# The light expert's folds one chunk later, and the job table made between the first gathers' rounds

## The reference, cut to what matters

```python
logits = (xt @ w_router).astype(jnp.float32)
top_v, top_i = lax.top_k(logits, TOP_K)            # 2 of 8
gates = jax.nn.softmax(top_v, axis=-1)
gate = jnp.sum(jax.nn.one_hot(top_i, N_EXPERTS) * gates[..., None], axis=1)
y = jnp.zeros_like(xt)
for e in range(N_EXPERTS):
    y = y + gate[:, e:e + 1] * ((jax.nn.silu(xt @ wg[e]) * (xt @ wu[e])) @ wd[e])
```

## Time and profile before

| | |
|---|---|
| median of 3 runs | 1616.9 us (1615.19 to 1618.0) |
| the profiled execution's own time | 1615.04 us |
| its span in the trace | 1613.2 us |
| PE busy | 1531.5 us, 95% |
| DVE busy | 1300.9 us, 81% |
| ACT busy | 1088.7 us, 67% |
| moved by DMA | 462.70 MB |
| expert pairs | from about 657 us to the end of the span |

### The profile page before, as it was taken

The page is one execution under the profiler, slowest core; times in us unless marked ns, Lnnn a source line. Parts: engine busy times, 40 slices in busy tenths (PEclk is TensorE's granted clock), DMA queues, the critical chain, the costliest instruction groups (busy, mean ns, idle before and its releaser), DMA issues.

```text
span 1613.2 us, 20830 instructions
## 1 busy us (share of the span) xinstructions
PE 1531.5 (95%) x7379; PEld 1257.6 (78%) x7379; DVE 1300.9 (81%) x1600; ACT 1088.7 (67%) x1423; POOL 119.8 (7%) x242
## 2 busy tenths in 40 slices
PE   6999999999999997799999899999999999999995
PEld 5888888888888886687777677787777787777884
DVE  5786676475554657689999999999999999999998
ACT  4664564645443463378888788878788877788884
POOL 3433332001000101000000000000000000000000
PEclk9999999999999999799999999999999999999998
DMA  9537444436465644399999999999999999999994
GB/s 344 201 131 218 147 139 150 170 98 216 144 200 179 212 134 145 99 319 383 383 388 398 362 380 386 387 364 401 381 385 386 393 362 397 366 386 387 397 377 182
DMA packets 203076, 462.70 MB, mean 287 GB/s; under 512 B 7902, under 2 KB 12396, under 8 KB 202844
## 3 DMA queue, kind: packets, MB, share of 16 engines
q1 hardware_dynamic: 200304, 454.32, 78.0%
q0 software_dynamic: 1904, 5.38, 1.3%
q10 hardware_dynamic: 764, 1.66, 0.3%
HBM read 460.29 MB, written 1.05 MB: 286 GB/s over the span
## 4 chain that ended last, share of the span: by engine, by line
PE 78%; ACT 8%; DVE 6%; issue 3%; DVEq 2%; DMA 2%; SPq 0%; ACTq 0%
PE ps L2027 8%; PE ps L2028 8%; PE ps L2029 8%; PE ps L2483 7%; PE ps L2485 7%; PE ps L2484 7%; PE ps L2498 7%; PE ps L2499 7%; ACT whi_sb L919 5%; PE ps L2536 4%; DVE wlo_sb L1268 2%; DMA raw_sb<-w_in 2%; PE ps L2445 1%; ACT gate_l_sb L1208 1%; PE ps L2073 1%
## 5 line engine op out<-in xcount | busy, mean ns | idle before, releaser
L1268 DVE TENSOR_TENSOR wlo_sb<-raw_sb,whi_sb 128x1024 fp32r<-128x1024 f32 x672 | 785.8, 1220 | 56.4 <-ACT whi_sb L919 52.4
L919 ACT ACTIVATE whi_sb<-raw_sb 128x1024 fp32r<-128x1024 f32 x672 | 668.0, 1051 | 178.6 <-PE ps L2499 88.3
L1260 DVE TENSOR_TENSOR wlo_sb<-raw_sb,whi_sb 128x1024 fp32r<-128x1024 f32 (+2 forms) x198 | 230.2, 1203 | 138.4 <-ACT whi_sb L911 137.3
L911 ACT ACTIVATE whi_sb<-raw_sb 128x1024 fp32r<-128x1024 f32 (+2 forms) x198 | 192.2, 1022 | 158.8 <-PE ps L2029 129.5
L2027 PE MATMUL ps<-whi_sb,xlo_sb 128*128 128x512 f32 (+2 forms) x544 | 212.4, 390 | 3.8 <-DVE xlo_sb L1307 3.4
L2029 PE MATMUL ps<-whi_sb,xhi_sb 128*128 128x512 f32 (+2 forms) x544 | 208.3, 383 | 0.0
L2028 PE MATMUL ps<-wlo_sb,xhi_sb 128*128 128x512 f32 (+2 forms) x544 | 208.2, 383 | 0.0
L2498 PE MATMUL ps<-whi_sb,xhi_sb 128*128 128x512 f32 x448 | 180.9, 404 | 0.0
L2483 PE MATMUL ps<-whi_sb,xlo_sb 128*128 128x512 f32 x448 | 177.4, 396 | 0.9 <-DVE xlo_sb L1818 0.7
L2499 PE MATMUL ps<-wlo_sb,xhi_sb 128*128 128x512 f32 x448 | 175.7, 392 | 0.0
L2485 PE MATMUL ps<-whi_sb,xhi_sb 128*128 128x512 f32 x448 | 175.3, 391 | 0.0
(11 more groups left out here) (378 smaller groups left out, 2109.6 us busy)
## 6 DMA issues: line engine op xcount, KB each, us to landing
raw_sb<-moe_wg SPq DMA_DIRECT2D x115, 1024.0 KB, 7.6
raw_sb<-moe_wu SPq DMA_DIRECT2D x112, 1024.0 KB, 7.6
raw_sb<-moe_wd SPq DMA_DIRECT2D x112, 1024.0 KB, 7.7
raw_sb<-w_in SPq DMA_DIRECT2D x40, 1024.0 KB, 5.1
raw_sb<-w_out SPq DMA_DIRECT2D x16, 1024.0 KB, 5.1
raw_sb<-ffn_wg SPq DMA_DIRECT2D x10, 1024.0 KB, 5.1
raw_sb<-ffn_wu SPq DMA_DIRECT2D x10, 1024.0 KB, 5.2
raw_sb<-ffn_wd SPq DMA_DIRECT2D x10, 1024.0 KB, 5.1
```

The lines of the kernel that those rows point to most:

```text
L911: nc.scalar.activation(whi[i % SPLIT][:, c:c + k // 2, 0:n], raw[i % RAW][:, c:c + k // 2, 0:n], ACT.Copy).then_inc(hi_ready, 1)
L919: nc.scalar.activation(whi[i % SPLIT][:, c:c + KC // 2, :], raw[i % RAW][:, c:c + KC // 2, :], ACT.Copy).then_inc(hi_ready, 1)
L1260: op = V.tensor_tensor(wlo[i % SPLIT][:, c:c + k // 2, 0:n], raw[i % RAW][:, c:c + k // 2, 0:n], whi[i % SPLIT][:, c:c + k // 2, 0:n], ALU ...
L1268: op = V.tensor_tensor(wlo[i % SPLIT][:, c:c + KC // 2, :], raw[i % RAW][:, c:c + KC // 2, :], whi[i % SPLIT][:, c:c + KC // 2, :], ALU.su ...
```

## The change

The folds of the light job move one step later, and with them what follows: the gate's fold from one to two steps after its last chunk, its silu from two to three, the value's fold from one to two, the product from two to three and the split from three to four. The heavy job's turn stays at one step, under the name `turn_h`. The gathers for the next pair start at step `up_end` + 5 instead of + 4; in the first pair this takes the heavy output's scatter, which comes at the earliest two steps after the last gather, from step 76 to 77. In ACT's code the silu stands ahead of the value's copy. `kinds`, `extras` and `table` leave the iterations of the first pair and go between the copies of the first gathers' rounds.

```diff
-Plan = namedtuple("Plan", "steps gate value fold_g silu_l after_value product_l split_l y_out pick gather back scat_l scat_h")
+Plan = namedtuple("Plan", "steps gate value turn_h fold_g silu_l fold_u product_l split_l y_out pick gather back scat_l scat_h")
...
-    gather = {up_end + 4 + r: r for r in range(ROUNDS)}
+    gather = {up_end + 5 + r: r for r in range(ROUNDS)}
     scat_h = max(min(y_out) + 2, max(gather) + 2)
-    return Plan(steps, both("g"), both("u"), ends(LIGHT_JOB, "g", 1), ends(LIGHT_JOB, "g", 2), both("u", 1),
-                ends(LIGHT_JOB, "u", 2), ends(LIGHT_JOB, "u", 3), y_out, up_end + 1, gather, LEAD if first else 6,
+    return Plan(steps, both("g"), both("u"), ends(HEAVY_JOB, "u", 1), ends(LIGHT_JOB, "g", 2), ends(LIGHT_JOB, "g", 3),
+                ends(LIGHT_JOB, "u", 2), ends(LIGHT_JOB, "u", 3), ends(LIGHT_JOB, "u", 4), y_out, up_end + 1, gather, LEAD if first else 6,
                 None if first else 1, scat_h)
...
-            for r in range(ROUNDS):
-                gathered(0, r)
-
...
+
+            kinds()
+            gathered(0, 0)
+            extras()
+            for r in range(1, ROUNDS):
+                gathered(0, r)
+            table()
...
                     if first(j):
-                        if i == 0:
-                            kinds()
-                        if i == 1:
-                            extras()
-                        if i == 2:
-                            table()
```

More of the change, by code:

```diff
@@ L231, in ends, with both @@
                 if s.b == b and s.chunk.which == which and s.chunk.last}
-    def both(which, later=0):
-        return tuple(ends(b, which, later) for b in (HEAVY_JOB, LIGHT_JOB))
+    def both(which):
+        return tuple(ends(b, which) for b in (HEAVY_JOB, LIGHT_JOB))
     up_end = max(max(ends(b, "u")) for b in (HEAVY_JOB, LIGHT_JOB))
     y_out = {i: b for b in (HEAVY_JOB, LIGHT_JOB) for i in ends(b, "d")}
-    gather = {up_end + 4 + r: r for r in range(ROUNDS)}
+    gather = {up_end + 5 + r: r for r in range(ROUNDS)}
     scat_h = max(min(y_out) + 2, max(gather) + 2)
-    return Plan(steps, both("g"), both("u"), ends(LIGHT_JOB, "g", 1), ends(LIGHT_JOB, "g", 2), both("u", 1),
-                ends(LIGHT_JOB, "u", 2), ends(LIGHT_JOB, "u", 3), y_out, up_end + 1, gather, LEAD if first else 6,
+    return Plan(steps, both("g"), both("u"), ends(HEAVY_JOB, "u", 1), ends(LIGHT_JOB, "g", 2), ends(LIGHT_JOB, "g", 3),
+                ends(LIGHT_JOB, "u", 2), ends(LIGHT_JOB, "u", 3), ends(LIGHT_JOB, "u", 4), y_out, up_end + 1, gather, LEAD if first else 6,
                 None if first else 1, scat_h)
@@ L1197, in pair @@
                         nc.scalar.activation(act_h[:, :], acc[:, HEAVY_JOB, 0, :], ACT.Silu).then_inc(hg_silu, 1)
-                    if i in plan.after_value[HEAVY_JOB]:
-                        p = plan.after_value[HEAVY_JOB][i]
+                    if i in plan.turn_h:
+                        p = plan.turn_h[i]
                         act.wait_ge(hT_ps, done + p + 1)
@@ L1208, in pair @@
                         nc.scalar.activation(gate_l[:, :], acc[:, LIGHT_JOB, 0, :], ACT.Copy).then_inc(lg_copied, 1)
+                    if i in plan.silu_l:
+                        p = plan.silu_l[i]
+                        act.wait_ge(lgT_ps, done + p + 1)
+                        if not first(j) or p:
+                            act.wait_ge(l_lo, done + p)
+                        nc.scalar.activation(actT_l[:, :], l_tp(p)[0], ACT.Silu).then_inc(l_silu, 1)
                     if i in plan.value[LIGHT_JOB]:
@@ L1214, in pair @@
                         nc.scalar.activation(value_l[:, :], acc[:, LIGHT_JOB, 1, :], ACT.Copy).then_inc(lu_copied, 1)
[L1215 to L1220, removed]
                     if i in plan.split_l:
@@ L2593, in pair @@
                         fold(l_tp(p)[0], gate_l).then_inc(lgT_ps, 1)
-                    if i in plan.after_value[LIGHT_JOB]:
-                        p = plan.after_value[LIGHT_JOB][i]
+                    if i in plan.fold_u:
+                        p = plan.fold_u[i]
                         pe.wait_ge(lu_copied, done + p + 1)
```

## The result

The changed kernel takes 1590.7 us (median of four runs, 1587.93 to 1591.36) against 1616.7 for the kernel before on the same chip. The ratio is 0.9833, interval 0.9821 to 0.9846: 26.0 us less, where 22.7 were forecast. The forecast of 1594.2 is 3.5 us too high. The median lies just under the forecast's own range of 1591 to 1598; 0.9833 of the 1616.9 us that the forecast started from is 1589.9, just under the wider one of 1590 to 1602. (The medians alone give 0.9839, inside the interval.) The sum came out nearly right, but two of its steps did not, and they have opposite signs.

What follows compares the result with a forecast made beforehand. PE, busy 95% of the span, was taken as the bound, with DVE close behind. Folds 15.5, job table 5.7 and pair starts 1.5 summed to 22.7 us, giving 1594.2 us; own range 1591 to 1598, 8-in-10 range 1590 to 1602.

Steps and rivals of the forecast that it cites:

- the folds' waits: Light job's folds: PE's waits for the gate's copy (15.1 us) and the value (0.4) vanish, 15.5 us won; bounds 0 to 15.5.
- pair starts: First fold of pairs two to four: waits for DVE's addition to `x`, 4.5 us in all, shrink; 1.5 us won.
- the transfers: Middle blocks: loads would supply 399 GB/s against 386 before, so a block stays at PE's 21.03 us.
- The 394 GB/s of rows 2: Two-block stretch, 21.01 us each, waits almost gone: its load rate was taken as evidence against transfers binding.
- Rival 3: Middle blocks: transfers bind at 386 GB/s, 21.74 us a block, only 0.1 us a block won; about 1608 us; chance 0.07.
- reserve of some 12 us: Load buffers: some 12 us between a buffer's release and ACT's need of its next content; a load lands in 7.5.
- The turn: Heavy job's turn: DVE's heavy product would be done some 0.5 us before the turn wants it, the block's nearest meeting.
- rival 4: Every block: light product and split delay DVE's heavy product, so the turn waits; slower, about 1627 us; chance 0.04.
- The first pair's table: First pair: moving the job table removes PE's 4.14 us wait and a 1.5 us slow clock; 5.7 us, bounds 3 to 6.
- rival 2: Pairs' starts: DVE catches up as PE no longer bunches steps, up to 3 us more won; about 1591 us; chance 0.09.

Runs made afterwards that it cites:

- the later turn: Changed kernel with the heavy job's turn two steps after its value's end instead of one: 1590.5 us with all loads, 1579.9 with half of each up chunk's rows loaded.
- wide loads: Changed kernel with up chunks loaded as 2 x 128 rows of 1024 columns, not 4 x 128 of 512 (other numbers): 1584.4 us; heavy turn at two steps, 1579.2.

## Why the prediction came out as it did

**The failed step is the size of the folds' waits**: "15.5 us", bounded by "no more than 15.5, since PE has little other idle there". It read PE's idle from the matmul records. A block went from 21.84 to 20.48 us once nothing waited (the runs with the later turn): 1.36 us, between the matmuls' 0.81 and the weight loads' 1.66 (1.22 + 0.44), and near the 1.43 that the starts of PE's instructions show. The first is too low, as a record's end covers the start of a wait; the second is too high by what the products before it still had to do, 0.27 us for the gate's fold (1.22 against 0.95). With the turn and the loads out of the way, folds and pair starts are worth 31 us: the 19.5 below and the 11.5 that lie between the changed kernel and the run with wide loads and the later turn. That takes the later turn to add nothing of its own. The kernel before had no such wait in its middle blocks, but it was not run with the later turn, so this is argued and not shown.

The Trainium skill, in "Perfetto Trace Analysis", Tensor Engine Instruction, says that the end of a TensorE record is estimated, not observed, and that PE can pull weight loads ahead of matmuls in flight. This case agrees: a block whose matmuls were "busy" 21.03 us was later done in 20.57 with the same products, and the timeline of the kernel before has weight loads that start inside the record of the product before them (1191.58 us, inside 1191.35 to 1191.74).

**The second failed step is the transfers**: "I keep the block at PE's 21.03". A block of 21.05 us, in the run with the value's fold back, asked for 399 GB/s too and got 386; the ring bore that almost without a price, but not the 408 of a block of 20.57. The 394 GB/s of rows 2 were no proof that up chunks can come faster. The loads issued in that stretch of the kernel before (809.21 to 851.24 us) are mostly down chunks, in rows of 1024 columns:

```profile
raw_sb<-moe_wd SPq DMA_DIRECT2D x10, 1024.0 KB, 7.9
raw_sb<-moe_wu SPq DMA_DIRECT2D x4, 1024.0 KB, 8.0
raw_sb<-moe_wg SPq DMA_DIRECT2D x2, 1024.0 KB, 7.8
```

Even this mixture has a cap: in the changed kernel the same two blocks (801.17 to 841.79 us) ask for 413 GB/s and move 398, while a load takes near 12 us to land. Rival 3 had the cap on the up chunks right (its 386, 387 here) and its price wrong. It reckoned each block at the rate of the loads, but the ring carries the deficit through the middle blocks, and only the last one or two of a pair pay: 6.3 us, not 14. The forecast's reserve of some 12 us held: ACT first waits for loads that take 12 to 13 us to land.

**The turn** was found to be the nearest meeting, with 0.5 us to spare, and rival 4 priced a wait there. It waits 0.29 us on the weight load in a middle block, and 1.1 to 1.6 in the last ones, where loads are late. Taking it away wins 5.2 us with wide loads and nothing with the real ones, since the time goes to the down steps instead.

**The first pair's table**: 5.7 forecast. From its first step to its eighth 26.59 us became 20.70, 5.9 less; the turn at 679.70 waits 0.27 us on the weight load and nothing on the matmul, and the clock stays at 1.00. The reckoned DVE times hold within 0.6 us (product forecast at 678.4, run at 678.97, in a stage that began 1.2 us later). What the table costs between the first gather and the first step stays open: 6.68 us in the changed kernel, but with the table elsewhere 6.38 in the run with the folds alone and 7.28 in the kernel before, whose granted clock there was 0.61 against 0.72 and 0.74. One slow stretch of the clock remains elsewhere, here behind a wait of 2.80 us at 888.49:

```profile
888.00:892.00 4.00, 3.51 (x9) 2.85 (x10) 4.00 (x5) 0.00 (x0) 0.00 (x0) 0.57 1.04 378
```

**The pair starts**: 1.5 us forecast, with a new wait of some 0.9 us for the first remainder in the third pair (1150.2 to 1151.1). The wait behind the first fold is there as foretold, but longer (1.26 on PE in the second pair):

```profile
911.42 0.50 PE L2481 MATMUL ps<-whi_sb,xlo_sb 128*128 128x512 f32 x1 [1.26 <-DVE wlo_sb L1268]
```

In the three pairs the 4.5 us of the fold's waits for `x` were replaced by 3.8 us of waits for `wlo`, and from the first gate fold of a pair to the second it takes 22.5 us where it took 22.2 to 22.3. No run separates this term from the folds', but nothing shows the 1.5 us, and rival 2, whose 1591 us came true, is not borne out in its reason.

Sum: 15.5 + 1.5 = 17.0 forecast, 19.5 measured in the trace (25.4 us less in the experts' stage, less 5.9). Of these, 18.9 lie in the 18 block intervals of the four pairs outside their first and last blocks (in the first pair all six count). By the account above 19.5 is 31 less 6.3 for the loads less 5.2 for the turn. Two errors, 14 us too little and 11.5 too much, nearly cancelled. That the sum came near is luck, not a sign that its terms were right.

## What to carry to other kernels

Price a short wait of PE from both rows: in the two blocks measured here the matmuls' idle was too low and the weight load's too high (0.81, 1.36 and 1.66 us; 0.3, 0.48 and 0.7), and waits of 0.4 us were missing from the first altogether (0.4 us in all against 12.2). The distance between the starts of PE's instructions gives the price itself. Before a faster stage is credited, compare the rate that it will ask for with the fastest rate that loads of that very shape have reached, and see which loads a stretch holds before taking its rate as proof. After the change, look at whether landing times grow from block to block: a ring with reserve shows no wait until its last blocks. And when several limits lie within a few per cent, moving one of them alone (the turn here) may show nothing.

## What the runs showed of the hardware

Loads of 1 MB as 4 x 128 rows of 512 float32 columns (pieces of 2 KB) moved 387 GB/s in middle blocks that asked for 408, as 2 x 128 rows of 1024 (4 KB) 409, at a DMA share of 1.05 and 1.03. The Trainium skill, in "DMA: Bandwidth & Descriptors", Why small descriptors are slow, gives a fixed cost of about 3 cycles a packet, beside one cycle for each 32 bytes in its example; an estimate from these figures is (128 + 3) / (2 x (64 + 3)), some 2% for the longer pieces. The direction agrees, the measured 5.7% is more than twice that, and no run here says what makes up the rest. Nor was a layout that gives the right weights in long rows tried: some 11 us under the changed kernel (1579.2) is what the later turn and such loads would bring, shown so far with other weights only.
